# Second attention of a two-block layer: values by head pairs into channels, gate by channels, weights divided in their step

## The chip, the cores and the metric

One Trainium2 chip, one of its cores. The metric is the device time of one execution in microseconds (us), the median of several; lower is better.

## The reference, cut to what matters

Two blocks of a layer run one after the other on a sequence of 256 tokens of width 1024: a state-space and attention mixer with a mixture of experts, and then a Hyena convolution beside a latent attention. The change lies in the attention of the second block:

```python
def dense_bidirectional_attention(q, k, v):      # 8 heads, 256 tokens, 96 wide; values 64 wide
    s = jnp.einsum('bhqd,bhkd->bhqk', qblk, kt).astype(jnp.float32) * scale
    p = jax.nn.softmax(s, axis=-1).astype(vt.dtype)
    return jnp.einsum('bhqk,bhkd->bqhd', p, vt)
...
u_attn = (attn * jax.nn.silu(z_attn)) @ w_attn_out[l]
merged = g_hy * u_hy + g_at * u_attn             # g_hy, g_at: sigmoid of the gates
x = x + merged @ w_out[l]
```

All of it is float32. `z_attn` and the gates are columns of one projection of the normalised x.

## The kernel before, in words

Each engine has its own program (`tensor`, `scalar`, `vector`, `gpsimd`, `sync`), an instruction queue in order; marks on semaphores tie them together (`mark`, `wait_ge`). No planner orders the work: the order is written out by hand, the same walk in each program.

**Weights.** Dense weights come in tiles of 128x2048 through six raw buffers (`raw`, fetched by SyncE once the tile six before is used). ScalarE copies a tile to a rounded high part (L1282) into one of four slots, which needs the tile four before to be used up; VectorE subtracts to get the low part (L1785). A product is then three matmuls, high by high, low by high, high by low (`mul3`, L521). Both splitting programs run up to three tiles ahead of the one in use (`Splitting.due`, L480): a new tile comes due when a `fill` reaches a new tile or ends a weight.

**Fillers.** Independent projections are cut in chunks (`gemm_chunk`, L530: both token tiles, six matmuls of 512 columns) and put between dependent work by `fill(n)`. In the attention loop 24 chunks wait: gate parts 2 and 3 (8 each), branch 0 and 1 (4 each). `fill` on TensorE (L549) takes two PSUM banks at the first chunk of a filler, banks 6 and 7 each time in this loop, and waits until their former content is drained; `fill` on VectorE (L1851) drains a gate part with bias and row scale at its last chunk (L1839, two operations, one for each bank), multiplies a branch by its gate (L1847), and splits tiles.

**Before the loop.** The attention gate `za` (L1344) is the first filler beside the Hyena transforms: tokens on partitions, drained by ScalarE with Silu and the row scale `rg` into `ZA`. VectorE works through the transforms' products, L2609 among them, and rotates queries (L2557 to L2563). GpSimd does only small powers (L2698).

**The loop (L1226, L1753, L2639), eleven steps h = 0 to 10.** TensorE: transposes of query and key of head h (`heads_T`); a chunk; scores of head h-1; a chunk; transposes of the exponentials of head h-2 (`weights2_T`, four); values of head h-3 (`values2`, four float32 products of 64 columns, eight pieces in the trace, into banks 4 and 5, which all heads share). ScalarE: `heads`, chunk, exponentials with their sums (L1748, two per head), chunk, and for odd h the drain of the transposed weights. VectorE: chunk, maximum (L2634) and scaled maximum (L2637), chunk, and for even h the drain of transposed weights (L1825). The sums are divided out behind the loop: reciprocals and a product with the two banks into `O2` (L2655), times `ZA` (L2659), eight transposes of `O2` on TensorE (L1240), a high part on ScalarE (L1300) and a low part on VectorE (L1815). Two branch chunks stand before and two behind these transposes. Then `wa2` follows (L1245), the merge of the branches, and `wo2`.

## Time and profile before

| | |
|---|---|
| median of 3 runs | 797.02 us (796.76 to 798.28) |
| the profiled execution | 796.26 us |
| its span in the trace | 794.5 us |
| TensorE matmul / weight load busy | 738.9 us (93%) / 557.4 us (70%) |
| VectorE / ScalarE / GpSimd busy | 465.0 us (59%) / 321.6 us (40%) / 17.9 us (2%) |
| granted TensorE clock, mean | 0.972 of full speed |

Engines in the rows: PE is TensorE (PEld its weight loads), DVE VectorE, ACT ScalarE, POOL GpSimd, SP SyncE. L519 is line 519 of the kernel. A TensorE row gives a matmul's start and its time to the end of its result; matmuls overlap, so the time for which one holds the engine is the distance to the next start. A float32 product shows as two pieces. Idle time in brackets is that of the engine before the operation, with what ended it.

### The profile page before, as it was taken

How to read it: one execution, taken by the hardware profiler on the slowest of the kernel's cores; microseconds unless marked ns; L12 is line 12 of the kernel's file. 1: busy time of each engine (PE TensorE's matmuls, PEld its weight loads, DVE VectorE, ACT ScalarE, POOL GpSimd, SP SyncE). 2: the span in 40 equal slices, each digit the busy share in tenths (PEclk: the TensorE clock that was granted, in tenths of full speed). 3: DMA queues.
4: the chain of work that ended last, by engine and by line, in shares of the span. 5: the costliest groups of instructions: out<-in, count | busy, mean ns of one | idle time of the engine just before them, and what ended most of it. 6: DMA issues, size and time to landing. Idle time of an engine off the chain costs nothing.

```text
span 794.5 us, 11035 instructions
## 1 busy us (share of the span) xinstructions
PE 738.9 (93%) x4636; PEld 557.4 (70%) x4636; DVE 465.0 (59%) x825; ACT 321.6 (40%) x479; POOL 17.9 (2%) x15
## 2 busy tenths in 40 slices
PE   7999999999999999996799798779999999999998
PEld 7978886888877886563345254337999966678886
DVE  6878965455766665531333221128777698875673
ACT  6464446536437225210111110127674634255631
POOL 0000000000000000000000000001100003000000
PEclk9999999999999999998879988899999999999999
DMA  9765542333439849899999999997453654433311
GB/s 314 238 206 185 163 158 104 106 107 106 139 110 410 294 189 422 315 366 420 419 421 417 421 421 421 419 398 268 148 197 120 214 184 160 156 109 106 106 53 54
DMA packets 63153, 189.97 MB, mean 239 GB/s; under 512 B 7481, under 2 KB 11835, under 8 KB 51132
## 3 DMA queue, kind: packets, MB, share of 16 engines
q1 hardware_dynamic: 61326, 184.44, 62.7%
q10 hardware_dynamic: 1774, 4.79, 1.8%
q8 instruction: 38, 0.62, 0.3%
q14 instruction: 15, 0.12, 0.0%
HBM read 188.16 MB, written 1.05 MB: 238 GB/s over the span
## 4 chain that ended last, share of the span: by engine, by line
PE 64%; DVE 14%; DMA 13%; ACT 6%; issue 2%; POOL 1%; SPq 0%; DVEq 0%; POOLq 0%
PE pb L519 60%; DMA raw<-in_w_exp_up 6%; DMA WHo<-in_w_exp_up 4%; DVE rawo L1785 4%; PE pb L528 4%; ACT WH L1282 2%; DMA WHo<-in_w_exp_down 1%; DVE cv_ L1893 1%; ACT arena L1441 1%; DVE arena L2054 1%; DMA X<-in_x 1%; POOL small L2690 1%; DVE arena L2100 0%; ACT arena L1476 0%; ACT arena L1310 0%
## 5 line engine op out<-in xcount | busy, mean ns | idle before, releaser
L1785 DVE TENSOR_TENSOR rawo<-raw,WH 128x2048 fp32r<-128x2048 f32 (+5 forms) x80 | 172.7, 2175 | 64.5 <-ACT WH L1282 64.4
L519 PE MATMUL pb<-WH,HTh 128*128 128x512 f32 (+2 forms) x384 | 155.0, 404 | 3.9 <-DVE rawo L1785 1.7
L1282 ACT ACTIVATE WH<-raw 128x2048 fp32r<-128x2048 f32 (+5 forms) x80 | 144.0, 1822 | 21.1 <-PE pb L519 15.1
L519 PE MATMUL pb<-rawo,HTh 128*128 128x512 f32 (+2 forms) x384 | 147.7, 385 | 0.0
L519 PE MATMUL pb<-WH,HTl 128*128 128x512 f32 (+2 forms) x384 | 147.5, 384 | 0.0
L519 PEld LDWEIGHTS pb<-WH,HTh 128*128 128x128 f32 x384 | 72.3, 188 | 22.5 <-issue 5.1
L519 PEld LDWEIGHTS pb<-rawo,HTh 128*128 128x128 f32 x384 | 72.2, 188 | 14.3
L519 PEld LDWEIGHTS pb<-WH,HTl 128*128 128x128 f32 x384 | 72.4, 188 | 13.0 <-issue 1.0
L519 PE MATMUL pb<-WH,arenao 128*128 128x512 f32 x192 | 59.7, 392 | 1.2 <-DVE arenao L1819 1.2
L519 PE MATMUL pb<-raw,arena 128*32 128x256 f32 (+1 forms) x256 | 49.7, 491 | 10.8 <-DMA raw<-in_w_exp_up 6.3
L519 PE MATMUL pb<-arena 128*32 128x256 f32 (+6 forms) x252 | 58.1, 429 | 1.6 <-ACT arena L1698 0.7
L2338 DVE TENSOR_TENSOR rt_<-rt_,pb 128x256 f32<-128x256 f32 x8 | 3.4, 421 | 89.8 <-ACT rt_ L1561 89.8
L519 PE MATMUL pb<-WHo,arena 128*32 128x256 f32 (+1 forms) x160 | 43.2, 504 | 7.6 <-DMA WHo<-in_w_exp_up 6.9
L519 PE MATMUL pb<-HTh,WH 128*128 128x256 f32 (+1 forms) x184 | 47.4, 284 | 0.0
L519 PE MATMUL pb<-HTh,rawo 128*128 128x256 f32 (+1 forms) x184 | 47.2, 283 | 0.0
L519 PE MATMUL pb<-HTl,WH 128*128 128x256 f32 (+1 forms) x184 | 47.1, 282 | 0.0
L519 PE MATMUL pb<-arena,rt_ 128*32 128x512 f32 (+1 forms) x208 | 44.6, 471 | 1.3 <-DVE arena L2028 0.6
L1561 ACT ACTIVATE rt_<-pb 128x256 f32<-128x256 f32 x8 | 3.1, 383 | 99.5 <-PE pb L519 99.5
L519 PEld LDWEIGHTS pb<-WH,arenao 128*128 128x128 f32 x192 | 35.7, 188 | 8.7 <-DVE rawo L1785 1.4
L519 PEld LDWEIGHTS pb<-arena 128*32 128x32 f32 (+4 forms) x252 | 27.5, 161 | 19.9 <-issue 8.8
L519 PEld LDWEIGHTS pb<-raw,arena 128*32 128x32 f32 (+1 forms) x256 | 20.5, 140 | 26.3 <-issue 13.3
L519 PE MATMUL pb<-rawo,arenao 128*128 128x512 f32 x96 | 37.4, 390 | 0.0
(363 smaller groups left out, 1266.2 us busy)
## 6 DMA issues: line engine op xcount, KB each, us to landing
raw<-in_w_in SPq DMA_DIRECT2D x46, 1024.0 KB, 5.1
raw<-in_w_exp_up SPq DMA_DIRECT2D x18, 1024.0 KB, 21.1
arena<-in_w_exp_gate SPq DMA_DIRECT2D x13, 1024.0 KB, 22.4
arena<-in_w_exp_down SPq DMA_DIRECT2D x12, 1024.0 KB, 15.8
WHo<-in_w_exp_down SPq DMA_DIRECT2D x9, 1024.0 KB, 23.5
raw<-in_w_out SPq DMA_DIRECT2D x8, 1024.0 KB, 5.2
raw<-in_w_exp_gate SPq DMA_DIRECT2D x8, 1024.0 KB, 16.0
WHo<-in_w_exp_up SPq DMA_DIRECT2D x8, 1024.0 KB, 21.4
```

The source lines that it names most:

```text
L519: return e.matmul(o, l, r, start=start, stop=stop, skip_group_check=True)
L528: return e.transpose(o, i, ident[0:k, 0:k])
L1282: e.activation(h_, r_, ACT.Copy).then_inc(hi.sem, hi.mark(k))
L1441: ins = e.activation(S1[s][:, cut], S1[s][:, cut], ACT.Exp, bias=nmx[:, s, t:t + 1], scale=-1.0, accum_out=ssum[:, t, h:h + 1])
L1561: e.activation(HG[q % 2], pb(("gu", q))[:, 0:256], ACT.Silu).then_inc(ac.sem, ac.mark(("su", q)))
L1785: e.tensor_tensor(l_, r_, h_.bitcast(F32), ALU.subtract).then_inc(lo.sem, lo.mark(k))
L1893: e.scalar_tensor_tensor(out=cv[:, s:L], in0=u[:, 0:L - s], scalar=cw[:, 3 - s, g:g + 1], in1=cv[:, s:L], op0=ALU.mult, op1=ALU.add).then_inc(
L2054: ins = e.scalar_tensor_tensor(out=LM[:, h, :], in0=pb(("lm", t, h0))[:, (h - h0) * 128:(h - h0) * 128 + 128], scalar=Ac[:, t, h:h + 1], i ...
L2338: e.tensor_tensor(HG[q % 2], HG[q % 2], pb(("gu", q))[:, 256:512], ALU.mult).then_inc(ve.sem, ve.mark(("gu", q)))
L2690: e.tensor_tensor(ss, ss, half, ALU.pow).then_inc(po.sem, po.mark(("rs", n)))
```

## The change

The division of the exponentials moves into the loop: VectorE does a reciprocal and two scalings per head (`shares2`) before their transposes. Values are computed two heads at a time with the values as the stationary side: four products of 256 columns, head 2p on output partitions 0 to 63 and head 2p+1 on 64 to 127, so the output is there by channels. The gate is made by channels as well (`channel_chunk`: four groups of 128 channels, three matmuls of 256 columns each, per chunk), drained plainly by ScalarE in two copies, multiplied on GpSimd by the row scale spread over the partitions (`RB`, whose place moves since it must live longer), and put through Silu by ScalarE in one operation of 128x1024. VectorE gates a pair (`output_gated`), ScalarE takes the high part (`output_high`), VectorE the low part (`output_low`). The output needs no transposes. Bank 4 alone holds the values; the fillers of the loop take banks 5 and 6, 7 and 5, 6 and 7 in turn. The rows of `wa2` are read in another order, in pieces of the same 2 KB.

```diff
--- before.py
+++ after.py
@@ -319,7 +319,7 @@
         FHID, FSU = (x[:, 0:512].rearrange("p (f l) -> p f l", f=2) for x in (rt_, sg_))
         NT = tuple(arena_r[:, o:o + 2048].rearrange("p (c l) -> p c l", c=8) for o in (0, 2048))
         RD = arena[:, 6144:6400].rearrange("p (t l) -> p t l", t=2)
-        RB = arena[:, 8192:8448]
+        RB = C["matt"][:, 0:256]
         XNs = [x.bitcast(F32) for x in (XNh, XNl)]
         gathers = lambda q: () if q in (0, 6, 7) else range(4) if q == 1 else (2 * (q % 2), 2 * (q % 2) + 1)
         by_chunk = lambda a: a.rearrange("p (c i) -> p c i", c=8)
@@ -340,12 +340,11 @@
         CQT = tuple(x[:, 0:768].rearrange("p (c l) -> p c l", c=3) for x in HD_)
         CKT = tuple(x[:, 768:1280].rearrange("p (c l) -> p c l", c=2) for x in HD_)
         UT = tuple(x[:, 0:1024].rearrange("p (c l) -> p c l", c=4) for x in HD_)
-        OT2 = tuple(x[:, 0:4, :] for x in HT)
+        OT2 = tuple(arena_r[:, o:o + 1024].rearrange("p (c l) -> p c l", c=4) for o in (8704, 9728))
         G1 = arena[:, C1:C1 + 2048].rearrange("p (t d) -> p t d", t=2)
         G2 = arena[:, 4096:6144].rearrange("p (t d) -> p t d", t=2)
         G_ = (G1, G2)
-        ZA = rt_[:, 0:1024].rearrange("p (t d) -> p t d", t=2)
-        O2 = rt_[:, 1024:2048].rearrange("p (t d) -> p t d", t=2)
+        ZAT, OG = (rt_[:, o:o + 1024].rearrange("p (c l) -> p c l", c=4) for o in (0, 1024))
         cqj = [sg_[:, 0:384], sg_[:, 384:768]]
         ckj = [sg_[:, 0:256], sg_[:, 384:640]]
         h8 = lambda a, d: a.rearrange("p (h d) -> p h d", d=d)
@@ -449,7 +448,7 @@
         weight("za", w2, 8, 2720, 512, "(c p)")
         for i in range(4):
             weight(("gate", i), w2, 8, 3232 + 512 * i, 512, "(c p)")
-        for key, w, kc, rows_ in (("whn", whn, 4, "(p c)"), ("wa2", wa2, 4, "(p c)"), ("wo2", wo2, 8, "(c p)")):
+        for key, w, kc, rows_ in (("whn", whn, 4, "(p c)"), ("wa2", wa2, 4, "(c p)"), ("wo2", wo2, 8, "(c p)")):
             for i in range(2):
                 weight((key, i), w, kc, 512 * i, 512, rows_)
 
@@ -544,15 +543,30 @@
                 for c in range(len(chunk_at[key])):
                     gemm_chunk(name, key, c, o, lhs, ready)
 
-            open_fill, fill_at = {}, deque([6])
+            open_fill, fill_at = {}, deque([(6, 7)])
+
+            def channel_chunk(name, key, c, o, lhs, ready):
+                k, j, last = chunk_at[key][c]
+                lo.wait_ge(e, k)
+                ve.wait_ge(e, (ready, c))
+                w = tuple(x[:, j, :] for x in tile_parts(k))
+                end = c == len(chunk_at[key]) - 1
+                for i in range(4):
+                    ins = mul3(o[i // 2][:, 256 * (i % 2):256 * (i % 2) + 256], tuple(x[:, 128 * i:128 * i + 128] for x in w),
+                               tuple(x[:, c, :] for x in lhs), c == 0 and i % 2 == 0, end)
+                if last:
+                    ins.then_inc(mm.sem, mm.mark(("tile", k), *([(name, 0), (name, 1)] if end else [])))
 
             def fill(n):
                 for name, c in todo.next(n):
                     key, lhs, ready, drainer, turned = fill_of[name]
                     if c == 0:
-                        open_fill[name] = [ring.take((name, t), drainer, at=fill_at[0] + t) for t in range(2)]
-                        fill_at.rotate(1)
-                    gemm_chunk(name, key, c, open_fill[name], lhs, ready, turned)
+                        open_fill[name] = [ring.take((name, t), drainer, at=fill_at[0][t]) for t in range(2)]
+                        fill_at.rotate(-1)
+                    if name == "za":
+                        channel_chunk(name, key, c, open_fill[name], lhs, ready)
+                    else:
+                        gemm_chunk(name, key, c, open_fill[name], lhs, ready, turned)
 
             def channels_by_part(key, names, ready, drainers, within):
                 o = [ring.take(name, by) for name, by in zip(names, drainers)]
@@ -1152,7 +1166,7 @@
             todo.add(("gate", 0), 8)
             todo.add(("gate", 1), 8)
             ring.of, ring.i = range(4), 0
-            fill_at.append(4)
+            fill_at.append((4, 5))
             for o_ in range(2):
                 for f in range(2):
                     for mat in ("fc", "fs"):
@@ -1187,8 +1201,7 @@
             todo.add(("branch", 0), 4)
             todo.add(("branch", 1), 4)
             fill_at.clear()
-            fill_at.append(6)
-            held_o2 = [ring.take(("o2", t), ve, at=4 + t) for t in range(2)]
+            fill_at.extend(((5, 6), (7, 5), (6, 7)))
 
             def heads_T(h):
                 o = ring.take(("hd", h), ac)
@@ -1207,21 +1220,25 @@
 
             def weights2_T(h):
                 o = ring.take(("p2", h), (ve, ac)[h % 2])
-                ac.wait_ge(e, ("s2", h))
-                for i in range(4):
-                    ins = turn(o[:, i * 128:i * 128 + 128], S2[:, h % 4, i * 128:i * 128 + 128])
+                ve.wait_ge(e, ("sn2", h))
+                for kk in range(2):
+                    for t in range(2):
+                        ins = turn(o[:, kk * 256 + t * 128:kk * 256 + t * 128 + 128],
+                                   S2[:, h % 4, t * 256 + kk * 128:t * 256 + kk * 128 + 128])
                 ins.then_inc(mm.sem, mm.mark(("p2", h)))
 
-            def values2(h):
-                (ve, ac)[h % 2].wait_ge(e, ("p2", h))
+            def values2(p):
+                o = ring.take(("o2", p), ve, at=4)
+                for h in (2 * p, 2 * p + 1):
+                    (ve, ac)[h % 2].wait_ge(e, ("p2", h))
                 ve.wait_ge(e, (("kv", 1), 0))
                 ac.wait_ge(e, (("kv", 1), 1))
-                for t in range(2):
-                    for kk in range(2):
-                        ins = mul(held_o2[t][:, h * 64:h * 64 + 64],
-                                  P2[h % 4][:, t * 256 + kk * 128:t * 256 + kk * 128 + 128],
-                                  V2[:, kk, h * 64:h * 64 + 64], kk == 0, kk == 1)
-                ins.then_inc(mm.sem, mm.mark(("pv2", h)))
+                for kk in range(2):
+                    for i in range(2):
+                        h = 2 * p + i
+                        ins = mul(o[64 * i:64 * i + 64, 0:256], V2[:, kk, h * 64:h * 64 + 64],
+                                  P2[h % 4][:, kk * 256:kk * 256 + 256], kk == 0, kk == 1)
+                ins.then_inc(mm.sem, mm.mark(("pv2", p)))
 
             for h in range(11):
                 if h < 8:
@@ -1233,11 +1250,8 @@
                     fill(1)
                 if 2 <= h <= 9:
                     weights2_T(h - 2)
-                if h >= 3:
-                    values2(h - 3)
-            fill(2)
-            ve.wait_ge(e, "o2")
-            transposed("o2T", lambda t: O2[:, t, :], 4)
+                if h >= 4 and h % 2 == 0:
+                    values2(h // 2 - 2)
             fill(99)
             ring.of, ring.i = range(8), 0
 
@@ -1342,7 +1356,10 @@
                     ve.wait_ge(e, "rt")
                     drain(name, ZH, ACT.Silu, by=rg_turned)
                 elif name == "za":
-                    drain(name, ZA, ACT.Silu, by=rg)
+                    for t in range(2):
+                        mm.wait_ge(e, (name, t))
+                        e.activation(ZAT[:, 2 * t:2 * t + 2, :], pb((name, t))[:, :].rearrange("p (c l) -> p c l", c=2),
+                                     ACT.Copy).then_inc(ac.sem, ac.mark((name, t)))
                 elif name[0] == "gate" and i < 2:
                     sigmoid(i)
                 weights(used(key))
@@ -1713,6 +1730,8 @@
             todo.add(("gate", 1), 8)
             fill(9)
             fill(4)
+            po.wait_ge(e, "za")
+            e.activation(ZAT, ZAT, ACT.Silu).then_inc(ac.sem, ac.mark("zas"))
             fill(4)
             fill(3)
             fill(2)
@@ -1750,6 +1769,10 @@
                                        accum_out=ssum[:, t, h:h + 1])
                 ins.then_inc(ac.sem, ac.mark(("s2", h)))
 
+            def output_high(p):
+                ve.wait_ge(e, ("og", p))
+                e.activation(OT2[0][:, p, :], OG[:, p, :], ACT.Copy).then_inc(ac.sem, ac.mark(("o2h", p)))
+
             for h in range(11):
                 if h < 8:
                     heads(h)
@@ -1758,13 +1781,15 @@
                     exps(h - 1)
                 if h < 9:
                     fill(1)
+                if h in (5, 7, 9):
+                    output_high((h - 5) // 2)
                 if 2 <= h <= 9 and h % 2:
                     if h >= 6:
-                        mm.wait_ge(e, ("pv2", h - 6))
+                        mm.wait_ge(e, ("pv2", (h - 6) // 2))
                     drain_t(("p2", h - 2), P2[(h - 2) % 4])
-            for i in (2, 3):
-                sigmoid(i)
-            high("o2T", OT2, 4, after=(("gate", 3), 1))
+            sigmoid(2)
+            output_high(3)
+            sigmoid(3)
             fill(99)
             weights(used(("wa2", 0)))
             high("m2T", UT, 4, after=(("branch", 1), 1))
@@ -2636,29 +2661,46 @@
                 ve.wait_ge(e, ("mr2", h))
                 e.tensor_tensor(nmx[:, s, :], mx[:, s, :], nhq[:, :, h], ALU.mult).then_inc(ve.sem, ve.mark(("mx2", h)))
 
+            def shares2(h):
+                s = h % 4
+                ac.wait_ge(e, ("s2", h))
+                e.reciprocal(rsum[:, :, h:h + 1], ssum[:, :, h:h + 1]).then_inc(ve.sem, ve.mark(("rs2", h)))
+                ve.wait_ge(e, ("rs2", h))
+                for t in range(2):
+                    cut = S2[:, s, t * 256:t * 256 + 256]
+                    ins = e.tensor_scalar(cut, cut, rsum[:, t, h:h + 1], None, ALU.mult)
+                ins.then_inc(ve.sem, ve.mark(("sn2", h)))
+
+            def output_gated(p):
+                mm.wait_ge(e, ("pv2", p))
+                ac.wait_ge(e, "zas")
+                e.tensor_tensor(OG[:, p, :], pb(("o2", p))[:, 0:256], ZAT[:, p, :], ALU.mult).then_inc(
+                    ve.sem, ve.mark(("og", p), ("o2", p)))
+
+            def output_low(p):
+                ac.wait_ge(e, ("o2h", p))
+                e.tensor_tensor(OT2[1][:, p, :], OG[:, p, :], OT2[0][:, p, :].bitcast(F32), ALU.subtract).then_inc(
+                    ve.sem, ve.mark(("o2T", p)))
+
             for h in range(11):
+                if h in (5, 7, 9):
+                    output_gated((h - 5) // 2)
                 fill(1, h < 10)
                 if 1 <= h <= 8:
                     scores2(h - 1)
                 if h < 9:
                     fill(1)
+                if 1 <= h <= 8:
+                    shares2(h - 1)
+                if h in (5, 7, 9):
+                    output_low((h - 5) // 2)
                 if 2 <= h <= 9 and h % 2 == 0:
                     if h >= 6:
-                        mm.wait_ge(e, ("pv2", h - 6))
+                        mm.wait_ge(e, ("pv2", (h - 6) // 2))
                     drain_t(("p2", h - 2), P2[(h - 2) % 4])
-            ac.wait_ge(e, ("s2", 7))
-            for t in range(2):
-                rs = rsum[:, t, 0:8]
-                e.reciprocal(rs, ssum[:, t, 0:8]).then_inc(ve.sem, ve.mark(("rs2", t)))
-                mm.wait_ge(e, ("pv2", 7))
-                ve.wait_ge(e, ("rs2", t))
-                e.tensor_tensor(hd(O2[:, t, :]), hd(pb(("o2", t))[:, :]), rs.unsqueeze(2).to_broadcast([128, 8, 64]),
-                                ALU.mult).then_inc(ve.sem, ve.mark(("o2", t)))
-                ac.wait_ge(e, ("za", t))
-                ve.wait_ge(e, ("o2", t))
-                e.tensor_tensor(O2[:, t, :], O2[:, t, :], ZA[:, t, :], ALU.mult).then_inc(ve.sem, own("o2"))
+            output_gated(3)
             weights(used(("whn", 0)))
-            low("o2T", OT2, 4)
+            output_low(3)
             fill(99)
             for i in range(2):
                 for t in range(2):
@@ -2696,6 +2738,9 @@
             for i in range(2):
                 ve.wait_ge(e, ("hs", i))
                 e.tensor_tensor(hs8[i], hs8[i], mh8, ALU.pow).then_inc(po.sem, po.mark(("hs", i)))
+            ve.wait_ge(e, "rb")
+            ac.wait_ge(e, ("za", 1))
+            e.tensor_tensor(ZAT, ZAT, RB.unsqueeze(1).to_broadcast([128, 4, 256]), ALU.mult).then_inc(po.sem, po.mark("za"))
 
 
         def sync(e):
```

## Rows read from the trace of the kernel before

**Rows 1.** Loop: us, then busy us (count) of PE, PEld, DVE, ACT, POOL; clock, DMA
```profile
698.40:756.59 58.19, 56.04 (x314) 47.63 (x312) 35.88 (x46) 36.73 (x69) 0.00 (x0) 1.00 0.33 109
```

**Rows 2.** TensorE timeline: start us, us, operation [idle before <- releaser]
```profile
700.11 0.47 PE L519 MATMUL pb<-WH,HTh 128*128 128x512 f32 x1 [1.11 <-DVE arena L1839]
...
738.88 0.47 PE L519 MATMUL pb<-WH,HDh 128*128 128x512 f32 x1 [0.27 <-DVE arena L1839]
...
749.62 0.47 PE L519 MATMUL pb<-WH,HDh 128*128 128x512 f32 x1 [0.59 <-DVE small L2652]
...
752.77 1.23 PE L528 MATMUL pb<-c,rt_ 128*128 128x128 f32 x8 [0.18 <-DVE rt_ L2659]
```

**Rows 3.** TensorE timeline, end of a step of the attention loop
```profile
715.64 0.60 PE L528 MATMUL pb<-c,XN 128*128 128x128 f32 x4
716.07 1.00 PE L519 MATMUL pb<-arena,sg_ 128*128 128x64 f32 x8
716.91 0.60 PE L528 MATMUL pb<-c,arena 128*96 128x128 f32 x4
```

**Rows 4.** TensorE timeline, expert stage, products for four column quarters
```profile
400.57 0.39 PE L519 MATMUL pb<-raw,arena 128*32 128x256 f32 x3
400.58 0.38 PE L519 MATMUL pb<-WHo,arena 128*32 128x256 f32 x1
400.79 0.39 PE L519 MATMUL pb<-raw,arena 128*32 128x256 f32 x3
```

**Rows 5.** TensorE timeline, first attention, two row halves
```profile
123.86 0.93 PE L519 MATMUL pb<-arena 64*128 64x128 f32 x8
...
125.05 0.39 PE L519 MATMUL pb<-WH,HTl 128*128 128x512 f32 x1
```

**Rows 6.** TensorE timeline, 256-wide and 512-wide products; the last two are 47 apart
```profile
600.11 0.28 PE L519 MATMUL pb<-HTh,rawo 128*128 128x256 f32 x1
600.23 0.28 PE L519 MATMUL pb<-HTl,WH 128*128 128x256 f32 x1
...
650.89 0.39 PE L519 MATMUL pb<-WH,HTl 128*128 128x512 f32 x1
...
661.56 0.39 PE L519 MATMUL pb<-WH,HTh 128*128 128x512 f32 x1
```

**Rows 7.** Timelines of VectorE, TensorE and ScalarE, 662 to 687
```profile
662.49 2.28 DVE L1785 TENSOR_TENSOR rawo<-raw,WH 128x2048 fp32r<-128x2048 f32 x1
...
670.65 1.29 DVE L2609 TENSOR_TENSOR arena<-pb,arena 128x512 f32<-128x512 f32 x2
...
671.58 0.39 PE L519 MATMUL pb<-rawo,HTh 128*128 128x512 f32 x1
...
686.39 1.29 ACT L1320 ACTIVATE arena<-arena 128x512 f32<-128x512 f32 x2 [17.96 <-DVE arena L1839]
```

**Rows 8.** Groups of VectorE: a scaling, a reciprocal, a product from PSUM (mean ns last)
```profile
L2452 DVE TENSOR_SCALAR arena<-arena,small 128x256 f32<-128x256 f32 x2 | 0.6, 350 | 0.8 <-POOL small L2690 0.8
...
L2272 DVE RECIPROCAL small<-small 128x2 f32<-128x2 f32 x1 | 0.2, 165 | 0.0
...
L2338 DVE TENSOR_TENSOR rt_<-rt_,pb 128x256 f32<-128x256 f32 x8 | 3.4, 421 | 89.8 <-ACT rt_ L1561 89.8
```

**Rows 9.** Timelines of VectorE and ScalarE, steps 2 and 3 of the loop
```profile
714.45 0.69 DVE L2634 TENSOR_REDUCE small<-pb 128x2 f32<-128x512 f32 x1 [0.32 <-PE pb L519]
...
718.42 2.29 DVE L1785 TENSOR_TENSOR rawo<-raw,WH 128x2048 fp32r<-128x2048 f32 x1 [1.10 <-ACT WH L1282]
...
715.38 0.56 ACT L1748 ACTIVATE XN<-pb,small 128x256 f32<-128x256 f32 x1
...
716.48 1.91 ACT L1282 ACTIVATE WH<-raw 128x2048 fp32r<-128x2048 f32 x1
```

**Rows 10.** Timeline of GpSimd (POOL)
```profile
659.41 2.90 POOL L2698 TENSOR_TENSOR small<-small 128x16 f32<-128x16 f32 x1 [45.57 <-DVE small L2534]
662.66 4.88 POOL L2698 TENSOR_TENSOR small<-small 128x16 f32<-128x16 f32 x1 [0.34 <-DVE small L2534]
```

## The prediction, made before the changed kernel ran

> **What bounds the kernel now.** I read the stretch that the change touches, from the first head of the second attention to the first matmul with `wa2`, by its busy times first: TensorE is busy 56.04 of 58.19 us, VectorE 35.88, ScalarE 36.73, at the full granted clock [rows 1]. So TensorE's queue sets the end, and the question is what the change takes from it and what it makes it wait for. Its own timeline shows four waits in the stretch [rows 2]: 1.11 us at 700.11 for VectorE to empty both banks of gate part 1, 0.27 at 738.88 for part 3, 0.59 at 749.62 for the first half of the Hyena branch, 0.18 at 752.77 for the gated output that is transposed there. Behind 756.59 TensorE has no wait up to its last matmul, so a shift of that point is a shift of the end; only the last residual and the store follow.
>
> **What TensorE gains.** In an undisturbed step the four transposes of a head's weights hold TensorE from 715.64 to 716.07, its `values2` from 716.07 to 716.91, 0.84 us [rows 3]; eight heads make 6.7. The new form has per pair of heads four products of 256 columns with 64 output partitions, in two column halves of the array. Its nearest row for sharing is the expert stage: four products for four column quarters start within 0.02 us of each other, the next four 0.215 later, so such quarters do run side by side and half of a float32 product of 256 columns costs 0.215 [rows 4]. A pair has 4 x 2 such halves, two at a time: 4 x 0.215 = 0.86. Entering and leaving a divided array is not free: in the first attention two row halves (8 pieces, by their columns 0.64 us when side by side) hold the engine from 123.86 to 125.05 less one wide matmul of 0.23, so 0.96, 0.3 more [rows 5]. I take 0.86 + 0.3 = 1.15 a pair, 4.6 in all, a gain of 2.1; the ends are 0.86 (gain 3.3) and 1.7, nothing side by side (8 x 0.215, no gain). The eight transposes of the output go; four hold the engine 0.43 (715.64 to 716.07), eight have their last result after 1.23 [rows 2, 3]: a gain of 1.0. Work of TensorE in the stretch: 3.1 less.
>
> The Trainium skill (TensorEngine Tiling (Array Packing), Performance Considerations and Key Properties) promises up to twofold speed for a stationary side of up to 64 columns, and says that a change of the tiling mode drains the engine, without a price. By the promise alone a pair would cost 0.86, and the sum below would be 0.6 us lower; the row of the row halves speaks for the drain.
>
> **What TensorE pays earlier.** The attention gate `za` is now made by channels: 96 products of 256 columns instead of 48 of 512. 256-wide ones follow each other by 0.12 us, 512-wide ones by (661.56 - 650.89)/47 = 0.227 [rows 6]. 96 x 0.12 = 11.5 against 10.9: +0.6. About 0.1 of it is free: the matmul of 671.58 lets TensorE go at 671.81, but what follows it needs VectorE's second L2609, done at 671.94 [rows 7]. Net +0.5. From there to 700 it is busy with its own work and the 0.5 is passed on.
>
> **What the other engines get.** Per head a reciprocal (0.165) and two scalings of 128x256 (0.35 each, the second starting some 0.08 before the first ends) are put on VectorE between the exponentials and the transposes: 0.8 us from start to signal [rows 8]. Eight heads: 6 us of VectorE time, which has 22 idle. Gating by pairs (0.42 for 128x256 from PSUM, [rows 8]), the high part on ScalarE and the low part on VectorE lie one to two steps behind and nothing waits for them; after the last pair TensorE still has four branch chunks, 24 matmuls of 0.227 us or 5.4, and the chain of three operations with VectorE's split among it needs about 3.5. So removing the tail (O2, 2.8 us of VectorE) is worth only its waits. The Silu of 128x1024 on ScalarE has 17.96 idle us around it [rows 7]. `wa2` in other row order reads pieces of the same 2 KB, six raw buffers ahead: nothing; should the order of pieces hurt, it is hidden by that lead.
>
> **Where the order bites.** VectorE's queue is in order, and `shares2(h)` stands after its second `fill`. Two things are queued with it. I walked the queues of the three engines through the stretch with the durations of the rows: a chunk is six matmuls of 0.227 and some 0.07 of changing over, 1.43; the scores four halves of 0.215, 0.86; transposes of weights 0.43. With the old program the walk meets the old waits within 0.2 us each and the start of `wa2` within 0.4. With the new program:
> - Step 2: the exponentials of head 1 are ready at 714.5. VectorE waits for them, scales (0.73 until the next can start), drains the transposed weights of head 0 (0.6), and only then takes the maximum of head 2, which stood at 714.45 [rows 9], at 715.8. TensorE waits 0.5 for the scaled head 1.
> - Step 3 has the last chunk of gate part 2. VectorE is done with the maximum and its product at 716.6 and has bank 5 drained (0.7) at 717.3. TensorE has no values in this step any more and wants bank 5 for gate part 3 at 716.3 (weights of head 1 from 715.3, heads of head 4): it waits 1.1 where it waited some 0.1 before. Turning three banks saves waiting for the second bank but not for the first.
> - In the same `fill` VectorE must split the next weight tile, for which ScalarE first has to copy it. ScalarE copies after the exponentials of head 2 (1.1 us from 715.38, now from 716.75; the copy took 1.91 from 716.48) [rows 9]: copied at 719.8, split (2.2 until the next can start) at 722.0, scaled at 722.8. TensorE is there after a chunk, the scores and a chunk from 717.4, at 721.1: 1.8 of waiting. Even on the old clock the split ends at 720.7 and the scaling would at 721.5.
> - Steps 7 and 8 repeat both (gate part 3, the tile after it): 1.2 and 1.8, and 0.2 for the last head. Heads 3 to 5 are scaled in time.
> - The wait at the start falls from 1.1 to 0.4, since only the first bank of gate part 1 is asked for; that at the branch (0.59) and the one for the output (0.18) go.
> By occupancy (each wait some 0.15 longer than the profile's idle time) the old waits are 2.7, the new ones 7.3: +4.6. With -3.1 of work the stretch is 1.5 longer. With 0.5 from the gate: **+2.0 us**. The sum goes on the profiled execution, 796.26 us (span 794.5): 798.3. The median of the runs shown is 797.02, 0.76 above it, so I predict 799.1.
>
> The bounds by the same walk: pairs at 0.86 give +1.0 for the stretch, at 1.7 +3.0; scaling at 0.6 a head gives +0.5, at 1.0 +2.5.
>
> **GpSimd.** The product of 128x1024 has no near row: its largest is the power of 128x16, 2.90 us, and the second one 4.88 [rows 10]. The second ran beside VectorE's split, which reads two inputs, and that split took its 2.28, as others do [rows 7, 9]. So when the two meet it is GpSimd that pays. The product would start when that power is done, at 667.5, beside the rotation of the queries. I take VectorE's loss as 0; its other bound is the power's own 2.90. GpSimd's own time may be five times those 2.90 before ScalarE's 17.96 idle us are used up, and costs nothing below that.
>
> The Trainium skill (GPSIMD Engine Reference) gives 4497 ns for a two-input operation of 2048 (Performance versus the Vector engine) and says that its memory interfaces are shared with VectorE, with contention when that reads two inputs (Specifications). It is the rule behind rival 4. From it an estimate of 2.3 us for 1024, and up to as much lost to VectorE; no run here shows such a product.
>
> **Rivals.** A difference of 0.2% is 1.6 us, about what a measurement of this kernel can tell from no change.
> 1. *The scaling finds its room* (the other side): if VectorE gets to `shares2` before TensorE does, because ScalarE's copy runs ahead of the exponentials, the waits in steps 3, 4, 7 and 8 fall away. Then -3.1 work, -2.1 of old waits, +0.5: -4.7, 792.3. It decides once the split of steps 3 and 7 ends before 720.3 on the old clock, 1.7 earlier than in my walk. For it: VectorE idles 38% of the stretch. Against: the order in the code puts the copy behind the exponentials. Chance 0.14.
> 2. *Scaling and pairs at their cheap ends*: walk +0.3 and +0.5 of gate, 797.8. For it: the quarters of the expert stage. Chance 0.18.
> 3. *The halves don't run side by side* (the order i inside kk is lost, or the engine drains between them): +3.0 + 0.5, 800.5. Against: the expert stage. 0.14.
> 4. *GpSimd holds VectorE up* in the rotation by 2.9: TensorE, 0.5 later itself, has 0.4 of cover before what needs L2609, so 2.5 more, +4.5: 801.6. Against: the split of 2.28 beside the power. 0.12.
> The forecast has 0.42, with its own range from +0.8 to +3.4.
>
> **How the numbers follow.** Slower by over 0.2% means above +1.6: rivals 3 and 4 and 0.30 of the forecast's 0.42, 0.56. Within: 0.12 of the forecast and rival 2, 0.30. Faster: rival 1, 0.14. The range from 796.3 to 801.8 leaves out rival 1 and the outer tails.
>
> **What would show it.** Right: TensorE idle for about 1 us before the first matmul of gate part 3 and of the branch, released by L1839, and for about 1.7 us before the transposes of heads 2 and 6, released by the new tensor_scalar; VectorE's split of the tile in steps 3 and 7 standing just ahead of them; a pair's values at 1.1 to 1.2; no transposes of `rt_`. Wrong: no waits ahead of those transposes (rival 1); eight value pieces one after another (3); L2609 ending later than 0.5 us after its old 671.94 (4).

## The result, and the profile after

| | before | after |
|---|---|---|
| median (range, runs) | 796.95 us (795.92 to 799.51, 9) | 799.93 us (799.08 to 802.27, 9) |
| ratio, 95% interval | | 1.004 (1.0025 to 1.0055) |
| profiled execution / span | 796.26 / 794.5 us | 799.08 / 797.0 us |
| TensorE matmul / VectorE / GpSimd busy | 738.9 / 465.0 / 17.9 us | 734.8 / 471.2 / 20.3 us |
| granted TensorE clock, mean | 0.972 | 0.976 |

The change makes the kernel 0.4% slower, 2.98 us by the medians. The forecast was 799.1 us, +2.0 on the profiled execution, slower with a chance of 0.56.

TensorE's first product of the Hyena transforms starts between 643.15 and 646.53 us in the profiled executions of the kernels here, a spread of 3.4 us from work that no edit touches; so I compare stages, each from the start of one row of TensorE to the start of another. **Stage 1** goes from that product (the row of 16 that waits 0.75 us for ScalarE) to the first head of the attention, **stage 2** from there to the first matmul with `wa2`, **stage 3** to the end. First before, for the one window that [rows 1] doesn't have, then after, by busy times (columns as in [rows 1]):

```profile
643.69:698.40 54.71, 54.69 (x201) 37.07 (x202) 48.58 (x81) 16.76 (x14) 7.78 (x2) 1.00 0.42 142
```

```profile
643.15:699.88 56.73, 55.35 (x248) 39.58 (x249) 50.70 (x81) 17.73 (x15) 10.16 (x3) 1.00 0.42 136
699.88:759.11 59.23, 53.54 (x274) 41.18 (x273) 40.00 (x70) 36.01 (x71) 0.00 (x0) 1.00 0.32 107
759.11:797.00 37.89, 34.63 (x161) 28.49 (x159) 20.59 (x22) 8.26 (x8) 0.00 (x0) 0.99 0.16 56
```

Stage 1 grew by 2.02 us, stage 2 by 1.04 (58.19 before [rows 1]), stage 3 not at all: +3.06, with the clock at full speed in both. In stage 2 TensorE's busy time fell by 2.50 and its idle time rose by 3.54. TensorE's timeline after shows where it idles; it answers to [rows 2]:

```profile
673.44 7.13 PE L518 MATMUL pb<-arena 128*128 128x512 f32 x16 [1.38 <-DVE arena L2634]
...
700.89 0.50 PE L518 MATMUL pb<-WH,HTh 128*128 128x512 f32 x1 [0.41 <-DVE arena L1864]
...
716.90 0.63 PE L527 MATMUL pb<-c,XN 128*128 128x128 f32 x4 [0.31 <-DVE XN L2671]
...
718.88 0.50 PE L518 MATMUL pb<-WH,HTh 128*128 128x512 f32 x1 [0.82 <-DVE arena L1864]
...
724.39 0.63 PE L527 MATMUL pb<-c,XN 128*128 128x128 f32 x4 [1.62 <-DVE XN L2671]
...
741.89 0.50 PE L518 MATMUL pb<-WH,HDh 128*128 128x512 f32 x1 [1.01 <-DVE arena L1864]
...
747.32 0.66 PE L527 MATMUL pb<-c,XN 128*128 128x128 f32 x4 [1.53 <-DVE XN L2671]
```

The six in stage 2 make 5.70 us where the four of [rows 2] made 2.15. L2671 is the scaling of a head, L1864 the drain of a gate part (L1839 before), L2634 the transforms' product (L2609 before). Why head 2 waits longest is read from ScalarE and then VectorE, in the steps that [rows 9] shows of before:

```profile
718.19 0.56 ACT L1767 ACTIVATE XN<-pb,small 128x256 f32<-128x256 f32 x1 [1.65 <-DVE small L2662]
...
719.29 1.91 ACT L1296 ACTIVATE WH<-raw 128x2048 fp32r<-128x2048 f32 x1
```

```profile
718.07 1.41 DVE L1864 SCALAR_TENSOR_TENSOR arena<-pb,small,arena 128x512 f32<-128x512 f32 x2
721.23 2.29 DVE L1810 TENSOR_TENSOR rawo<-raw,WH 128x2048 fp32r<-128x2048 f32 x1 [1.75 <-ACT WH L1296]
...
723.63 0.62 DVE L2671 TENSOR_SCALAR XN<-XN,small 128x256 f32<-128x256 f32 x2
```

The exponentials of head 2 come at 718.19, behind them the copy of a weight tile; VectorE, which has that tile's split next, idles 1.75 us for it, splits, and only then scales head 2, whose exponentials were done when the copy began.

The first of TensorE's rows, in stage 1, was foreseen by rival 4 alone. Its cause stands in the timelines of GpSimd and VectorE after:

```profile
666.96 2.41 POOL L2743 TENSOR_TENSOR rt_<-rt_,c 128x1024 f32<-128x1024 f32 x1
```

```profile
666.95 0.17 DVE L2564 TENSOR_SCALAR small<-small 128x16 f32<-128x16 f32 x1
667.15 2.25 DVE L2566 TENSOR_SCALAR small<-small 128x16 f32<-128x16 f32 x1
669.32 0.28 DVE L2582 TENSOR_TENSOR cv_<-arena 128x128 f32<-128x128 f32 x1
...
672.10 1.29 DVE L2634 TENSOR_TENSOR arena<-pb,arena 128x512 f32<-128x512 f32 x2
```

A scaling of 128x16, whose twin just before takes 0.17 us, lasts 2.25 beside GpSimd's product and ends with it. VectorE comes 2.1 us late to L2634 (counted against run 5 below, where it isn't held).

### The profile page after: what moved, and what is told of

It is laid out like the page before. It is cut to its first block, busy times and chain, and to the rows that moved or that the text cites. A ratio compares the mean times of both kernels' runs of the same rounds, so it can differ in the third digit from the quotient of the medians.

```text
span 797.0 us, 11080 instructions
## 1 busy us (share of the span) xinstructions
PE 734.8 (92%) x4644; PEld 552.0 (69%) x4644; DVE 471.2 (59%) x849; ACT 322.6 (40%) x482; POOL 20.3 (3%) x16
## 4 chain that ended last, share of the span: by engine, by line
PE 54%; DVE 19%; DMA 15%; ACT 9%; issue 2%; POOL 1%; SPq 0%; DVEq 0%; POOLq 0%
PE pb L518 51%; DMA WHo<-in_w_exp_up 7%; DMA raw<-in_w_exp_up 6%; DVE rawo L1810 6%; ACT WH L1296 4%; PE pb L527 3%; DVE cv_ L1918 1%; DMA WHo<-in_w_exp_down 1%; ACT XN L1767 1%; ACT arena L1458 1%; DVE arena L2079 1%; DMA X<-in_x 1%; POOL small L2732 1%; DVE small L2659 0%; DVE arena L2125 0%
## 5 line engine op out<-in xcount | busy, mean ns | idle before, releaser
L518 PE MATMUL pb<-WH,HTh 128*128 128x512 f32 (+2 forms) x352 | 142.1, 404 | 4.0 <-DVE rawo L1810 1.7
L518 PE MATMUL pb<-rawo,HTh 128*128 128x512 f32 (+2 forms) x352 | 135.3, 384 | 0.0
L518 PE MATMUL pb<-WH,HTl 128*128 128x512 f32 (+2 forms) x352 | 135.0, 383 | 0.0
L518 PEld LDWEIGHTS pb<-WH,HTh 128*128 128x128 f32 x352 | 66.3, 188 | 21.3 <-issue 4.9
L518 PEld LDWEIGHTS pb<-rawo,HTh 128*128 128x128 f32 x352 | 66.1, 188 | 13.0
L518 PE MATMUL pb<-WH,arenao 128*128 128x512 f32 x224 | 69.6, 392 | 1.2 <-DVE arenao L1844 1.2
L518 PE MATMUL pb<-HTh,WH 128*128 128x256 f32 (+1 forms) x216 | 56.8, 286 | 0.0
L518 PE MATMUL pb<-HTh,rawo 128*128 128x256 f32 (+1 forms) x216 | 56.2, 283 | 0.0
L518 PE MATMUL pb<-HTl,WH 128*128 128x256 f32 (+1 forms) x216 | 56.1, 282 | 0.0
L518 PE MATMUL pb<-rawo,arenao 128*128 128x512 f32 x112 | 43.7, 390 | 0.0
L518 PEld LDWEIGHTS pb<-raw,arena 128*32 128x32 f32 (+1 forms) x256 | 20.3, 142 | 29.5 <-issue 13.4
```

What stands on the lines that cost most here:

```text
L518: return e.matmul(o, l, r, start=start, stop=stop, skip_group_check=True)
```

## The experiments

| kernel | median, us | before in the same call | ratio (95%) | stage 1 | stage 2 |
|---|---|---|---|---|---|
| before | 796.95 | | | 54.71 | 58.19 |
| after | 799.93 | 796.95 | 1.004 (1.0025 to 1.0055) | 56.73 | 59.23 |
| 1 product a little later | 800.52 | 796.49 | 1.0057 (1.0037 to 1.0077) | 56.85 | 59.20 |
| 2 splits behind the scaling | 795.98 | 796.49 | 0.9987 (0.9974 to 0.9999) | 56.72 | 55.28 |
| 3 both, 1 and 2 | 796.77 | 796.49 | 0.9991 (0.9977 to 1.0005) | 56.88 | 55.30 |
| 4 no division | 793.52 | 796.49 | 0.996 (0.9946 to 0.9975) | 56.71 | 53.58 |
| 5 product behind the rotation | 799.49 | 797.98 | 1.0021 (1.0007 to 1.0035) | 55.05 | 59.23 |
| 6 no product | 799.78 | 797.98 | 1.0025 (1.0011 to 1.0039) | 55.05 | 59.20 |
| 7 four banks in turn | 801.28 | 797.98 | 1.0057 (1.0037 to 1.0077) | 56.72 | 59.24 |
| 8 edits 2 and 5 | 796.02 | 797.98 | 0.9981 (0.9968 to 0.9995) | 55.05 | 55.30 |
| 9 edit 8, one more chunk in step 9 | 795.53 | 796.98 | 0.9975 (0.996 to 0.9991) | 55.05 | 55.10 |
| 10 banks 6 and 7 | 800.36 | 796.98 | 1.0042 (1.0025 to 1.0058) | 56.74 | 60.06 |
| 11 pair's order (one run) | 799.45 | 796.98 | | 56.72 | 59.25 |
| 12 one column half (one run) | 802.47 | 796.14 | | 56.71 | 61.60 |

All start from the changed kernel; stage 3 is 37.8 or 37.9 in each. Stages 1 and 2 repeat within 0.06 us where an edit doesn't touch them, far closer than the medians, so what an edit is worth is read from the stages. Runs 11 and 12 rest on one execution each.

**1. GpSimd's product a little later.**

```diff
             ve.wait_ge(e, "rb")
+            ve.wait_ge(e, "hq")
```

> GpSimd's product waits for VectorE's two small scalings of the query factors. Theory: only VectorE's tensor_scalar is held up by the product (2.25 us for 128x16 in the changed kernel, 0.17 before), its two-input operations are not. Then the product runs beside the rotation (0.28 us each) at no cost, L2634 ends 2.1 us earlier, TensorE's wait of 1.38 us ahead of the second set of transform products goes down to under 0.1: 1.4 us less than the changed kernel, about 798.5 against 799.9. Rival (the product holds up every VectorE operation with two inputs, as the page on GpSimd has it): the rotation beside the product takes up to 2.4 us longer, the wait stays between 1 and 1.4, the time stays within 0.4 of the changed kernel.

The rival was right: stage 1 is as long as before the edit. GpSimd, then VectorE:

```profile
667.76 2.39 POOL L2744 TENSOR_TENSOR rt_<-rt_,c 128x1024 f32<-128x1024 f32 x1 [0.42 <-DVE small L2566]
```

```profile
667.51 0.17 DVE L2566 TENSOR_SCALAR small<-small 128x16 f32<-128x16 f32 x1
667.60 0.28 DVE L2582 TENSOR_TENSOR cv_<-arena 128x128 f32<-128x128 f32 x1
667.80 2.51 DVE L2583 TENSOR_TENSOR cv_<-arena 128x128 f32<-128x128 f32 x1
```

The small scaling is free again, and the first operation of the rotation that starts behind the product is held instead, 2.51 us where its neighbour takes 0.28. Here the victim is the next operation that VectorE starts once the product runs, and the loss is about the length of the product. The expectation's theory, that only a scaling is held, is refuted.

**2. VectorE splits behind the scaling.**

```diff
-                fill(1, h < 10)
+                fill(1, False, False)
...
-                    fill(1)
+                    fill(1, False, False)
...
+                if h < 9:
+                    name, c = steps[2 * h + 1]
+                    key = fill_of[name][0]
+                    weights(used(key) if c == len(chunk_at[key]) - 1 else used_before(key, c))
```

(`steps` is the list of chunks; the new lines stand at the end of the step, behind `shares2` and the drain.)

> In the attention loop VectorE splits the next weight tile at the end of a step, behind the maximum, the scaling and the drain, not within the chunks. Same operations, other order. Theory (the order of VectorE's queue costs the time): the waits of 1.62 and 1.53 us ahead of the transposes of heads 2 and 6 go; by the same walk of the queues about 1.5 appears ahead of the last head's transposes, and the two waits for a bank fall from 0.82 and 1.01 to about 0.6 and 0.4. The loop is 3 to 4 us shorter: 796 to 797. Rival (VectorE's added load costs the time, wherever it stands): no more than 0.5 us less than 799.9, the waits move to other heads.

Stage 2 falls by 3.95 us. VectorE's timeline in steps 2 and 3, then TensorE's waits:

```profile
718.57 1.41 DVE L1864 SCALAR_TENSOR_TENSOR arena<-pb,small,arena 128x512 f32<-128x512 f32 x2
719.93 0.17 DVE L2667 RECIPROCAL small<-small 128x2 f32<-128x2 f32 x1
720.13 0.61 DVE L2671 TENSOR_SCALAR XN<-XN,small 128x256 f32<-128x256 f32 x2
721.73 2.29 DVE L1810 TENSOR_TENSOR rawo<-raw,WH 128x2048 fp32r<-128x2048 f32 x1 [0.98 <-ACT WH L1296]
```

```profile
719.38 0.50 PE L518 MATMUL pb<-WH,HTh 128*128 128x512 f32 x1 [0.56 <-DVE arena L1864]
...
740.00 0.50 PE L518 MATMUL pb<-WH,HDh 128*128 128x512 f32 x1 [0.41 <-DVE arena L1864]
...
747.96 0.66 PE L527 MATMUL pb<-c,XN 128*128 128x128 f32 x4 [1.02 <-DVE XN L2671]
```

The scaling now stands ahead of the split that waits for ScalarE's copy, and the waits before heads 2 and 6 are gone; one of 1.02 us came before the last head, where 1.5 was expected. The same two scalings per head are still there: the 3.95 us came from the order of VectorE's queue, not from their work. No run gives the kernel before this order, so what it would gain there is open.

**3. Both.** The edits of 1 and 2.

> The product later and the splits later. Theory: the two stretches lie one behind the other on TensorE's path, so the gains add: 4.5 to 5.3 us less than the changed kernel, 794.6 to 795.4, under the kernel before (797.0). Rival: either gain is taken back in the other stretch, and the time is that of the better of the two alone.

Stage 1 is as in 1 and stage 2 as in 2. Nothing is gained beside 2 alone, as 1 gains nothing; the expected sum of two gains fails with 1.

**4. No division.** This kernel leaves the division of the exponentials out.

```diff
-                ve.wait_ge(e, ("sn2", h))
+                ac.wait_ge(e, ("s2", h))
...
-                if 1 <= h <= 8:
-                    shares2(h - 1)
```

> Leaves out the division of the exponentials: no reciprocals, no scalings, TensorE's transposes wait for ScalarE's exponentials alone. All else as in the changed kernel. Theory: the division where it stands costs what the walk gives, 6.2 us: no wait ahead of the transposes of heads 1, 2, 6, 7, bank waits of 0 to 0.4; 793.7. Rival (the waits come mostly from the new bank order and from the values' new form): 1 to 2 us less than 799.9 and waits of a bank of about 1 us remain.

Stage 2 is 53.58, 5.65 shorter. Two waits are left with a releaser in TensorE's timeline, both for the drain of a gate part:

```profile
703.00 0.50 PE L518 MATMUL pb<-WH,HTh 128*128 128x512 f32 x1 [0.41 <-DVE arena L1864]
...
740.26 0.50 PE L518 MATMUL pb<-WH,HDh 128*128 128x512 f32 x1 [0.41 <-DVE arena L1864]
```

So everything else of the change, with no division behind the loop either, is worth 58.19 - 53.58 = 4.6 us to the loop, and the division in its place costs 5.65. Of those, 4.88 are idle time (5.70 less 0.82).

**5. GpSimd's product behind the rotation**, started only when both of VectorE's L2634 are done.

```diff
             ve.wait_ge(e, "rb")
+            ve.wait_ge(e, ("ui", 0, 1))
```

> GpSimd's product waits for VectorE's second L2634 (the first order's gated transform), where TensorE has its next wait on VectorE only 14 us later and with 2.7 us to spare. Theory as the last run left it: the product and a VectorE operation that reads two inputs from memory exclude each other for the whole of the one that came first (2.25 us for a scaling of 0.17, 2.51 for a product of 0.28), operations with one input from PSUM are free. Then the product stands first behind the split (so it shows about 4.5 us), VectorE loses up to 2.4 us behind it, nothing in TensorE's path feels it, and TensorE's wait of 1.38 us goes to under 0.1: 1.4 us less than the changed kernel, about 798.5. Rival (the 0.6 us of the wider set of matmuls and VectorE's own chain make the wait, not the product): the wait stays above 0.5.

Stage 1 falls by 1.68 to 55.05, and the wait of 1.38 is gone. GpSimd, then VectorE:

```profile
673.74 4.34 POOL L2744 TENSOR_TENSOR rt_<-rt_,c 128x1024 f32<-128x1024 f32 x1 [4.40 <-DVE arena L2634]
```

```profile
673.58 2.28 DVE L1810 TENSOR_TENSOR rawo<-raw,WH 128x2048 fp32r<-128x2048 f32 x1
676.16 0.69 DVE L2604 TENSOR_TENSOR XN<-pb,arena 128x512 f32<-128x512 f32 x1 [0.30 <-PE pb L518]
677.88 0.69 DVE L2606 TENSOR_TENSOR sg_<-pb,arena 128x512 f32<-128x512 f32 x1 [1.02 <-PE pb L518]
```

Here VectorE's split came first and GpSimd paid: 4.34 us, the 2.1 that the split still had and 2.2 behind it, near its own 2.4. VectorE lost nothing: its next operations, with one input in PSUM, ran beside the rest of the product at their usual 0.69.

**6. No product.** This kernel leaves GpSimd's product out, so the gate isn't scaled by row; ScalarE's Silu waits for its own copies (`ac.wait_ge(e, ("za", 1))`).

> Leaves out GpSimd's product of the gate with the row scale; the Silu waits for ScalarE's copies. Theory: as in the run with the product behind L2634, the wait of 1.38 us goes and 1.4 us are gained, no more: 798.5. VectorE's second query scaling takes 0.17 us again. Rival: the wait stays.

Both stages are those of 5 within 0.03. In a place where VectorE has a split already under way and then operations with an input in PSUM, the product costs nothing; the 1.68 us were its place.

**7. Four banks in turn.**

```diff
-            fill_at.extend(((5, 6), (7, 5), (6, 7)))
+            fill_at.extend(((5, 6), (7, 4), (6, 7), (4, 6)))
...
-                o = ring.take(("o2", p), ve, at=4)
+                o = ring.take(("o2", p), ve, at=5)
```

> Gate part 3 takes banks 7 and 4, which are both free, and the values bank 5. Theory (both waits of step 3 and 4 come from the one queue of VectorE, and the later one takes over what the earlier gives up): the wait of 0.82 us ahead of gate part 3 goes, the one ahead of the transposes of head 2 grows from 1.62 to 2.6, the time stays within 0.4 of the changed kernel. Rival (the waits are independent): 0.8 to 1.0 us less, the wait at head 2 stays 1.6.

```profile
718.11 0.63 PE L527 MATMUL pb<-c,XN 128*128 128x128 f32 x4 [0.32 <-DVE XN L2671]
...
725.59 0.63 PE L527 MATMUL pb<-c,XN 128*128 128x128 f32 x4 [2.70 <-DVE XN L2671]
```

The wait of 0.82 between these two is gone, and that before head 2 grew from 1.62 to 2.70: stage 2 as it was. The wait taken away stood ahead of a later one of the same chain, and only moved.

**8. The edits of 2 and 5.**

> Splits at the end of a step, and the product behind L2634. Theory: both gains add, about 3.4 from the loop as measured and 1.4 from the product: 795.0 to 795.4, one to two us under the kernel before. Rival: 796 as with the late splits alone.

Stage 1 as in 5, stage 2 as in 2: 2.55 us less than before the change in all. By the medians it is 0.2% faster than the kernel before, and that interval (0.9968 to 0.9995) leaves 1 out.

**9. One more chunk in step 9.** The kernel of 8, with `if h < 9` ahead of the second `fill` made `if h < 10` on all three engines.

> The kernel of e8 with one more chunk of branch 0 in step 9, ahead of the transposes of the last head (the loop then runs out of chunks one earlier behind it). Theory (each wait is the distance between VectorE's scaled head and TensorE's arrival, so a chunk of 1.43 us put ahead of it absorbs the wait of about 1.0 before the transposes of the last head, and what it takes away behind the loop uncovers a bank wait of branch 1 of 0.5 to 0.9): the wait of 1.0 falls below 0.15, the stage from the first head to the first wa2 product 0.2 to 0.5 us shorter than e8's 55.30. Rival (the queue in order shifts VectorE's own work by as much, so the wait stays or only moves): the stage within 0.15 of 55.30 or longer.

```profile
717.33 0.50 PE L518 MATMUL pb<-WH,HTh 128*128 128x512 f32 x1 [0.56 <-DVE arena L1864]
...
737.97 0.50 PE L518 MATMUL pb<-WH,HDh 128*128 128x512 f32 x1 [0.41 <-DVE arena L1864]
...
747.46 0.50 PE L518 MATMUL pb<-WH,HDh 128*128 128x512 f32 x1 [0.73 <-DVE arena L1872]
```

The wait of 0.99 before the last head is gone, one of 0.73 for a bank came, and stage 2 is 0.20 shorter, at the lower end of what was expected. The medians of 8 and 9 don't tell them apart (0.9981 and 0.9975).

**10. Fillers on banks 6 and 7 each time.**

```diff
-            fill_at.extend(((5, 6), (7, 5), (6, 7)))
+            fill_at.append((6, 7))
```

> The changed kernel with its fillers back on banks 6 and 7 each time, in place of the turn 5/6, 7/5, 6/7. My walk's theory: the first product of gate part 1 waits for both banks again (1.1 us in place of 0.41), gate part 3 and branch 0 about 1.5 in place of 0.8 and 1.0, but the waits for the scaled heads 2 and 6 shrink by as much as TensorE comes later to them (1.6 and 1.5 fall to about 0.95), so the stage is 59.9 +- 0.3 against 59.23: the turning of the banks is worth 0.7 us. Rival (bank waits add up in full, the turning is worth some 1.9): stage 61.0 or more and the waits for heads 2 and 6 unchanged. Second rival (as with four banks, the time behind the scaled heads is fixed and the banks are worth nothing): stage within 0.15 of 59.23.

```profile
701.86 0.47 PE L518 MATMUL pb<-WH,HTh 128*128 128x512 f32 x1 [1.11 <-DVE arena L1864]
...
720.20 0.47 PE L518 MATMUL pb<-WH,HTh 128*128 128x512 f32 x1 [1.53 <-DVE arena L1864]
...
725.01 0.63 PE L527 MATMUL pb<-c,XN 128*128 128x128 f32 x4 [0.96 <-DVE XN L2671]
```

Stage 2 is 60.06: turning the banks is worth 0.83 us. The waits for banks and for scaled heads trade as the walk had it.

**11 and 12. What lets the values run two at a time.** In 11 the two loops of `values2` change places, so that both products of a head come before those of the next. In 12 both heads of a pair are put on output partitions 0 to 63, so partitions 64 to 127 of the attention output aren't computed:

```diff
-                        ins = mul(o[64 * i:64 * i + 64, 0:256], V2[:, kk, h * 64:h * 64 + 64],
+                        ins = mul(o[0:64, 256 * i:256 * i + 256], V2[:, kk, h * 64:h * 64 + 64],
```

> The changed kernel with head inside (i outside, kk inside) in the values of a pair: the two pieces of one column half follow each other, and only then the two of the other half. Theory A (the queue starts a piece as soon as its own column half is free, in order): about 0.215 for each same-half piece, so the distance from a pair's start to the next operation rises from 1.01 to 1.5 to 1.75 us, over four pairs 2 to 3 us, of which one half or more is given back where a scaled head is waited for behind it. Theory B (pieces of different halves don't overlap at all, the 1.01 is the plain pace): the distance stays at 1.01 within 0.05. The result is the same numbers either way.

> The changed kernel with both heads of a pair on output partitions 0 to 63 (one column half), the second head in columns 256 to 511 of the same bank; the other half stands idle, so partitions 64 to 127 of the attention output are not computed. In the run with head outside the pair kept its 1.02 us, so the order of the pieces is not what lets them run two at a time. Theory A (two pieces run side by side only where they lie in different column halves, and the queue finds them in either order): here nothing can overlap, the distance from a pair's start to the next operation rises from 1.01 to 1.6 to 1.8 us (8 x 0.215). Theory B (a piece of 256 columns of these products simply takes about 0.11, or the two pieces of one product run together, and the halves give nothing): the distance stays at 1.01 within 0.05.

The first pair of values and what follows it, on TensorE, after the change, in 11 and in 12:

```profile
724.95 1.08 PE L518 MATMUL pb<-sg_,arena 128*64 128x256 f32 x8
725.96 0.64 PE L527 MATMUL pb<-c,arena 128*96 128x128 f32 x4
```

```profile
725.26 1.09 PE L518 MATMUL pb<-sg_,arena 128*64 128x256 f32 x8
726.28 0.64 PE L527 MATMUL pb<-c,arena 128*96 128x128 f32 x4
```

```profile
725.97 1.94 PE L518 MATMUL pb<-sg_,arena 128*64 128x256 f32 x8
727.84 0.64 PE L527 MATMUL pb<-c,arena 128*96 128x128 f32 x4
```

From start to start a pair takes 1.01, 1.02 and 1.87 us. In one column half nothing overlaps, and in two halves the pieces run two at a time whatever their order. The two halves are worth 0.86 us a pair; of the 3.44 for four pairs 2.37 arrive in stage 2, since the later TensorE waits less for a bank (0.41 for 1.01), for head 6 (1.29 for 1.53) and for the last head. Theory A of 11, a price for its order, is refuted by 11, and both theories B, no overlap or no use of the halves, by 12. How the queue finds the partner in the order of 11 is open.

## Why the prediction was right, and the one step that failed

- **The loop was forecast at +1.5 and came to +1.04.** All its waits stand where the walk put them, released by what it named. To compare in the prediction's occupancy I take, at each wait, the distance from one start to the next less the smallest such distance between the same two kinds of operation in the loop. Forecast against measured: start 0.4, 0.66 (0.41 as idle time); head 1 0.5, 0.54; gate part 3 1.1, 1.12; head 2 1.8, 1.80; step 7 1.2, 1.26; step 8 1.8, 1.74; the last head 0.2, 0.19. The last has no idle time in brackets and is the distance of 0.35 before its transposes (0.23 elsewhere) and that of 0.42 behind them (0.35 elsewhere):

```profile
750.19 0.40 PE L518 MATMUL pb<-rawo,HDh 128*128 128x512 f32 x1
750.54 0.66 PE L527 MATMUL pb<-c,XN 128*128 128x128 f32 x4
750.96 0.47 PE L518 MATMUL pb<-WH,HDh 128*128 128x512 f32 x1
```

- Together they are 7.3, as forecast, though the prediction's own list adds up to 7.0 only. What was off is the other side: by the same measure the old waits are 3.1, not 2.7, 0.16 of them at 717.42, where the profile names no wait. So waiting grew by 4.2 and not by 4.6, which is nearly all of the 0.46 between forecast and stage. Run 10 shows that the walk was right for other banks too, runs 2 and 4 that the waits come from the scaling behind the split.
- **TensorE's work.** The gain was forecast at 3.1 and is 4.2 less 1.04, 3.2. A pair was put at 1.15 us, and that is what it takes where nothing is waited for: it holds TensorE for 1.01, the transposes ahead of it for 0.53 where those of [rows 3] take 0.43, and the operation behind it for 0.40, which takes 0.36 elsewhere:

```profile
734.61 0.60 PE L527 MATMUL pb<-c,XN 128*128 128x128 f32 x4
735.14 1.08 PE L518 MATMUL pb<-cv_,arena 128*64 128x256 f32 x8
736.15 0.64 PE L527 MATMUL pb<-c,arena 128*96 128x128 f32 x4
```

- Rival 3 (the halves don't run side by side) is what run 12 made of it, and not what the kernel does.
- The prediction set the promise of the Trainium skill (TensorEngine Tiling (Array Packing), Performance Considerations) at 0.86 a pair against 1.15. Between the halves twofold holds: 0.86 of 1.87 is saved, half of eight times 0.215. The rest, 0.29 a pair, is there in one half too (1.87 for 8 x 0.215, and the same 0.53 and 0.40 beside it), so it isn't the price of sharing. It is in line with the drain at a change of mode that the page (Key Properties) names without a price; no run isolates that.
- **The gate by channels was forecast at +0.6, net +0.5.** The stretch of its products lasts 11.90 us (649.72 to 661.62) where it lasted 11.30 (650.26 to 661.56): +0.60. Net it is +0.34 (55.05 of runs 5 and 6 less 54.71): the old slack hid more than the 0.1 I gave it.
- **The division, rival 1.** The loop without the scaling's waits is what rival 1 described, -5.2 in the loop and -4.7 with the gate. Run 4, without division, has -4.6 in the loop, and run 2, with all the work, -2.9 (55.28 for 58.19). So part of the other side can be had by a change of order in the code. It is another way than the condition that I named: there the split of steps 3 and 7 ends earlier, in run 2 it stands behind the scaling. In the change as written neither was so.
- **What failed: "I take VectorE's loss as 0"** for GpSimd's product. It was 2.1 us, and 1.68 of them reached TensorE (run 5), 1.38 of that seen as idle time; the rest was covered, as rival 4 had it with 0.4. Rival 4 had the place and the mechanism and put the loss at 2.9, the power's length; the product takes 2.41. The step that led astray is the reading of [rows 7, 10], "when the two meet it is GpSimd that pays". The split had begun before the power there, and that row fits as well with the rule that runs 1 and 5 show for the product: the one that comes first keeps the other out to its own end. The power's 4.88 against 2.90 fits 1.98 of waiting for the split's last 2.1, as in run 5; no run takes the split away to show it.
- The Trainium skill has this rule on a page that I hadn't set beside the rows: SBUF — State Buffer, section "SBUF: two separate sides", calls the pair of ports that VectorE and GpSimd share an exclusive lock, held by whichever starts first for the whole instruction. For the product the traces agree: 2.25 and 2.51 for VectorE, 4.34 for GpSimd. For the power they don't: VectorE's second split started while it ran and wasn't held (2.29, last section), so the rule doesn't hold for every operation of GpSimd over its whole time. The product's own length, which the prediction took from the Trainium skill's GPSIMD Engine Reference (Performance versus the Vector engine) as an estimate of 2.3 us, was about right (2.41).
- **The sum.** +1.5 and +0.5 were forecast. The stages show +1.04, +0.34 and +1.68, 3.06. Without the product's 1.68 it would have been +1.4, within 0.2% of before. The loop and the gate were put 0.6 too high and the product 1.7 too low, and the errors partly cancel. That the kernel is slower by more than 0.2%, as forecast, rests on the term that I put at 0: that much was luck.

## What to carry to other kernels

Work that is put on a half-idle engine can cost more by its place in that engine's queue than by its length: here 0.8 us a head on a VectorE idle for 38% cost 5.65, and 3.95 of it came back when an operation that waits for a third engine was moved behind it. Before a large two-input product goes to GpSimd, read VectorE's timeline beside it and give it a stretch where VectorE's operations have an input in PSUM; here it then cost nothing, and in the rotation 1.7. And when two rows show who pays in a meeting, look at who started first before making a priority of it.

## What the runs showed of the hardware

- GpSimd's product of 128x1024 and VectorE's operations in SBUF alone kept each other out until the one that had begun was done. It didn't take two inputs on VectorE's side: a scaling of 128x16, 0.17 us by itself, took 2.25. Operations with one input in PSUM weren't held (0.69 beside the product in run 5). Nor was the second split of 128x2048, after the change at 664.74 with its usual 2.29, though it began while GpSimd's power of 128x16 (662.12, 4.88) was still under way; what sets the power apart from the product, none of the runs tells.
- Products of 64 stationary columns ran two at a time in two column halves in either order of issue (1.01 and 1.02 us a pair), and one at a time in one half (1.87). Either way a pair made the operations beside it 0.14 us longer (0.53 for 0.43, 0.40 for 0.36).
